# All gathered expert rows on VectorE, the dot rows first, and a row in every second group left over

## What is computed

```
q = (xb @ w_q).reshape(blk, PEER_HEADS, 2, PEER_QDIM // 2)
s = einsum("thpd,pnd->thpn", q, keys)
sv, si = top_k(s, 16)
cand = sv[:, :, 0, :, None] + sv[:, :, 1, None, :]
cidx = si[:, :, 0, :, None] * 128 + si[:, :, 1, None, :]
best, pos = top_k(cand.reshape(...), 16)
eidx = take_along_axis(cidx..., pos)
g = softmax(best)
act = gelu(einsum("thkd,td->thk", u_tab[eidx], xb))
y = einsum("thk,thkd->td", g * act, v_tab[eidx])
```

## Time and profile before

| | |
|---|---|
| median of 3 runs | 5243.1 us (5241.55 to 5251.99) |
| the profiled execution's own time | 5246.87 us |
| its span | 5245.1 us |
| TensorE busy | 92% of the span |
| VectorE busy | 56% |
| ScalarE busy | 20% |
| GpSimd busy | 35% |
| mean DMA rate | 284 GB/s |

### The profile page before, as it was taken

One profiled execution on the slowest core, in us unless ns is written; L12 is line 12 of the kernel. 1 busy time (PEld: TensorE's weight loads), 2 busy tenths in 40 slices (PEclk: granted clock), 3 DMA queues, 4 the chain that ended last, 5 costly groups with the idle time before them and its releaser, 6 DMA issues.

```text
span 5245.1 us, 84061 instructions
## 1 busy us (share of the span) xinstructions
PE 4838.5 (92%) x25356; PEld 3800.1 (72%) x25356; DVE 2943.4 (56%) x5545; ACT 1067.2 (20%) x2624; POOL 1860.3 (35%) x2605
## 2 busy tenths in 40 slices
PE   7999899788999988999989998987889999989998
PEld 5887776567877765777768877764678777757776
DVE  2543332424789787666436433323348896876664
ACT  1112111210111367100011121112101114680000
POOL 4430000324554445454245200003236543454442
PEclk9999999889999999999999999998999999999999
DMA  7753679487789999999877437895768898989997
GB/s 275 246 177 115 201 239 320 139 263 241 266 304 339 342 366 329 383 409 412 328 274 245 164 114 219 250 308 159 249 212 297 307 344 335 377 321 391 413 405 283
DMA packets 723471, 1489.24 MB, mean 284 GB/s; under 512 B 64592, under 2 KB 405584, under 8 KB 721568
## 3 DMA queue, kind: packets, MB, share of 16 engines
q0 software_dynamic: 249888, 858.18, 44.5%
q1 hardware_dynamic: 473216, 626.61, 35.9%
HBM read 1315.99 MB, written 302.75 MB: 309 GB/s over the span
## 4 chain that ended last, share of the span: by engine, by line
PE 61%; DMA 13%; issue 9%; DVE 8%; DVEq 3%; SPq 2%; POOLq 2%; POOL 1%; ACT 1%; ACTq 0%
PE PS L1357 19%; PE PS L694 10%; PE PS L798 8%; DMA xT<-u_rows,arena 6%; PE PS L1232 3%; PE PS L1300 3%; PE PS L925 3%; DVE xT L1960 2%; PE PS L1251 2%; PE PS L1256 2%; DMA hT<-u_rows,arena 1%; PE PS L837 1%; DMA xT<-v_rows,arena 1%; DMA u_rows<-arena 1%; DVE arena L1995 1%
## 5 line engine op out<-in xcount | busy, mean ns | idle before, releaser
L1300 PE MATMUL PS<-hT,ring 128*128 128x288 f32 x4096 | 1014.5, 408 | 17.0 <-DMA ring<-in_uv 17.0
L1357 PE MATMUL PS<-arena,ring 128*128 128x288 f32 x4096 | 994.5, 406 | 1.0 <-DMA ring<-in_uv 1.0
L1300 PEld LDWEIGHTS PS<-hT,ring 128*128 128x128 f32 x4096 | 775.2, 191 | 224.9 <-issue 17.9
L1357 PEld LDWEIGHTS PS<-arena,ring 128*128 128x128 f32 x4096 | 778.2, 190 | 217.0 <-DMA ring<-in_uv 1.9
L565 POOL DMA_DIRECT2D u_rows<-arena x1024 | 564.5, 553 | 144.5 <-DVE arena L1507 63.6
L798 PE MATMUL PS<-hT,ring 128*128 128x272 f32 x2304 | 604.6, 409 | 5.9 <-DMA ring<-in_wst 5.9
L673 POOL DMA_INDIRECT xT<-u_rows,arena x410 | 416.4, 1016 | 457.9 <-DVE arena L1960 386.2
L1969 DVE SCALAR_TENSOR_TENSOR PS<-xT,arena,PS 128x1024 f32<-128x1024 f32 x344 | 443.4, 1289 | 215.4 <-DMA xT<-v_rows,arena 205.2
L1960 DVE CUSTOM_DVE_ANT_0 xT<-xT,PS 128x1024 f32<-128x1024 f32 x410 | 495.0, 1216 | 104.6 <-DMA xT<-u_rows,arena 103.8
L2178 ACT ACTIVATE arena<-PS 128x272 f32<-128x272 f32 (+12 forms) x540 | 207.6, 395 | 1520.1 <-PE PS L798 533.5
L798 PEld LDWEIGHTS PS<-hT,ring 128*128 128x128 f32 x2304 | 438.6, 198 | 99.0 <-issue 16.6
(11 more groups left out here) (399 smaller groups left out, 5920.9 us busy)
## 6 DMA issues: line engine op xcount, KB each, us to landing
ring<-in_uv SPq DMA_DIRECT2D x512, 512.0 KB, 6.4
ring<-in_wst SPq DMA_DIRECT2D x312, 512.0 KB, 5.5
u_rows<-arena POOLq DMA_DIRECT2D x1024, 128.0 KB, 4.6
v_rows<-in_uv SPq DMA_DIRECT2D x256, 512.0 KB, 6.6
arena<-in_uv POOLq DMA_DIRECT2D x216, 512.0 KB, 6.2
arena<-in_ck SPq DMA_DIRECT2D x128, 256.0 KB, 5.1
arena<-in_cvv POOLq DMA_DIRECT2D x64, 256.0 KB, 4.3
hT<-in_cvv POOLq DMA_DIRECT2D x64, 256.0 KB, 5.5
```

What stands on the lines that cost most here:

```text
L1300: i = mm(PS[:, 2 + s % 2, 0:TD], ring[:, s, c, :], hD[:, c, :], start=(c == 0), stop=(c == DC - 1))
L1357: i = mm(PS[:, 2 + b, 0:TD], ring[:, s, j, :], WB[:, row, :], start=(row == 0), stop=(row == NK - 1))
```

## The change

Three things are changed, all in PEER and the same in both layers.

1. `T_ROWS` is gone: TensorE treats no gathered row, ScalarE makes no diagonal, and the order of the rows is simply all u rows of block 0, all of block 1, then all v rows of block 0 and of block 1. All 512 are VectorE's.
2. Beside the U pass, VectorE's comparison for the next group stands right behind `weighted` of this one, ahead of the gathered rows that follow it.
3. In the 28 groups left over VectorE does one row in every second group: 14 rows in all, where there were 28 on VectorE and 28 on TensorE.

```diff
-    order = u[0] + u[1][:N_EARLY]
-    for g in range(N_LEFT):
-        order += [v[0][g], u[1][N_EARLY + g]]
-    return order + u[1][N_EARLY + N_LEFT:] + v[0][N_LEFT:] + v[1]
+    return u[0] + u[1] + v[0] + v[1]
...
                 if n >= NBUF:
-                    used = row_t if on_tensor(n - NBUF) else row_v
-                    g.wait_ge(used.sem, used.at(l, RANK[n - NBUF]))
+                    g.wait_ge(row_v.sem, row_v.at(l, n - NBUF + 1))
...
             for g in range(N_IN_U, N_OH):
                 one_hots(g)
-                r = g - N_IN_U
-                n = T_ROWS[r]
-                pe.wait_ge(row_ld[n % NBUF].sem, row_ld[n % NBUF].at(l, 16 * (n // NBUF + 1)))
-                pe.nop(nofuse=True)
-                pe.wait_ge(dg_s.sem, dg_s.at(l, r + 1))
-                pe.nop(nofuse=True)
-                for hf in range(2):
-                    i = mm(HTK[0][:, hf, :], DG[r % 2], row_buf(n)[:, hf * 512:(hf + 1) * 512], start=(r == 0), stop=(r == N_LEFT - 1))
-                i.then_inc(row_t.sem, 1)
...
+            onehots(0)
             for m in range(I_OH, NK):
                 g = m - I_OH
-                onehots(g)
                 rows(first + (P + N_EARLY - first) * (2 * g + 1) // (2 * N_IN_U))
...
                 weighted(g, m)
+                onehots(g + 1)
                 rows(first + (P + N_EARLY - first) * (2 * g + 2) // (2 * N_IN_U))
-            v.wait_ge(dot_s.sem, dot_s.at(l, 1))
-            v.nop(nofuse=True)
-            tt(DOT[:, 0:P], DOT[:, 0:P], GW[:, 0:P], ALU.mult)
-            v.drain().then_inc(dot_v.sem, 1)
-            onehots(N_IN_U)
             for g in range(N_IN_U, N_OH):
                 if g + 1 < N_OH:
                     onehots(g + 1)
                 weighted(g, NK - 1)
-                row()
+                if g % 2:
+                    row()
...
-            rows(RANK[N_SW + NBUF + 1])
+            rows(N_SW + NBUF + 2)
...
             row_onehots(N_IN_U)
             row_onehots(N_IN_U + 1)
-            s_.wait_ge(dot_v.sem, dot_v.at(l, 1))
-            for r in range(N_LEFT):
-                if 0 < r < N_LEFT - 1:
-                    row_onehots(N_IN_U + r + 1)
-                if r >= 2:
-                    s_.wait_ge(row_t.sem, row_t.at(l, r - 1))
-                act(DG[r % 2], ident[:, :], ACT.Copy, scale=DOT[:, r:r + 1]).then_inc(dg_s.sem, 1)
+            for g in range(N_IN_U + 2, N_OH):
+                row_onehots(g)
             activated(1)
```

More of the change, by code:

```diff
@@ L173 @@
 N_IN_U = NK - I_OH
-N_LEFT = N_OH - N_IN_U
 ROWS = row_order()
@@ L177 @@
 N_SW = (NROW - 12) // NBUF * NBUF
[L178 to L182, removed]
+LAST = {key: max(n for n, r in enumerate(ROWS) if r[:2] == key) + 1 for key in (("u", 0), ("u", 1), ("v", 0))}
 def shape_constants():
@@ L282, in build @@
     row_buf = lambda n: (ROW_X if n < N_SW else ROW_W)[n % NBUF]
-    DG = [xflat[:, 4 * DM + P * i:4 * DM + P * (i + 1)] for i in range(2)]
     YD = [hflat[:, TD * c:TD * (c + 1)] for c in range(DC - 1)]
@@ L411, in build @@
     row_ld = [Sig(f"expert_row_loaded{b}", 16 * len(range(b, NROW, NBUF))) for b in range(NBUF)]
-    row_v, row_t = Sig("row_used_by_vector", len(V_ROWS)), Sig("row_used_by_tensor", len(T_ROWS))
-    dot_s, dot_v, dg_s = Sig("dots_activated", 2), Sig("first_row_weights_ready", 1), Sig("row_diagonal_ready", N_LEFT)
+    row_v = Sig("row_used", NROW)
+    dot_s = Sig("dots_activated", 2)
     xk_st, xr_ld = Sig("x_kept", 16), Sig("x_loaded_again", 16)
@@ L1946, in row @@
                 nonlocal at
-                n = V_ROWS[at]
+                n = at
                 at += 1
@@ L1963, in row @@
                 else:
-                    if blk == 0 and k == N_LEFT:
-                        v.wait_ge(row_t.sem, row_t.at(l, N_LEFT))
-                        v.nop(nofuse=True)
                     v.wait_ge(row_v.sem, row_v.at(l, at - 1))
@@ L2162, in _ @@
                 v.drain()
-                rows(min(at + 1, len(V_ROWS)))
+                rows(min(at + 1, NROW))
             gathered_out(0)
-            rows(len(V_ROWS))
+            rows(NROW)
             v.drain().then_inc(ya_v.sem, 1)
@@ L2441, in activated @@
                 cols = slice(GCOL[blk], GCOL[blk] + P)
-                s_.wait_ge(row_v.sem, row_v.at(l, LAST_DOT[blk]))
+                s_.wait_ge(row_v.sem, row_v.at(l, LAST["u", blk]))
                 act(DOT[:, cols], DOT[:, cols], ACT.Gelu_apprx_tanh).then_inc(dot_s.sem, 1)
@@ L2462, in _ @@
                 dense_kept(c)
-            s_.wait_ge(row_v.sem, row_v.at(l, RANK[ROWS.index(("v", 0, P - 1))]))
+            s_.wait_ge(row_v.sem, row_v.at(l, LAST["v", 0]))
             copy(YT[0], htk(0)).then_inc(ya_s.sem, 1)
```

## The result

The changed kernel takes 5288.8 us (median of 4 runs, 5285.8 to 5296.9), the one before, run beside it, 5246.8 us (5241.6 to 5252.0): a ratio of 1.0089, 95% interval 1.0077 to 1.0102. It is slower by about 42 us. Its profiled execution took 5291.5 us, with a span of 5289.9 us.

What follows compares the result with a forecast made beforehand. TensorE was taken to bound the kernel, except where it waits for weights and gathered rows. Per layer -16 + 2 - 3 + 38 = +21, twice +42, plus 1 for the second layer's clock: 5286 us, 8-in-10 range 5250 to 5312.

Steps and rivals of the forecast that it cites:

- The groups left over: Stage between U and V pass: at ScalarE's pace of 2.89 us a group, the V pass begins 15.9 us earlier, -16 a layer.
- the rival of hand-overs at the lower clock: Groups left over: hand-overs between three engines set the 3.36 us pace, so the stage gets no shorter, 5314 us; chance 0.10.
- the comparison ... is ready before ScalarE's factor: First group left over: VectorE's comparison, moved ahead of two rows, comes early, so ScalarE is the last to arrive.
- some 82 us: Sign in the later profile: V pass begins this long behind the U pass's end, where it was 101.7 us.
- TensorE's clock: V pass's beginning: TensorE stays at the lower clock through the groups left over, costing half of about 4 us, +2 a layer.
- Beside the U pass: During the U pass: comparison ahead of the rows saves little, -3 a layer, with bounds 0 and -22.
- takes away what TensorE waits for: Beside the U pass: the moved comparison removes TensorE's waits for it, at most 21.9 us a layer.
- its doubt behind it: Beside the U pass: VectorE still has the same rows, each behind its transfer, so only its wait for ScalarE's copy is saved.
- The rows that are moved: V pass and layer's end: 267 rows instead of 226, row 500 done at V + 505, layer ends V + 540, +38.
- The early signals: V pass: row 384 at V + 288, needed by V + 312, hidden by 24 us; TensorE stalls from 2.07 us a row.
- go round as fast as loaded DMA engines let them: V pass: loaded DMA engines limit how fast the five row buffers are reused, at 1.914 us a row.
- The break-even of 1.81 us: V pass: pace per row at which row 500 is done at V + 484, where the change neither gains nor loses.

Runs made afterwards that it cites:

- e11: e6 with eight more 128 x 128 products on TensorE, result unread, behind the one-hot products of each group left over: 5215.1 us, ratio 0.9928 to the kernel before.
- e6: Changed kernel with 42 rows on VectorE among the groups left over, where it had 14: 5215.7 us, ratio 0.9944 to the kernel before.
- e1: Kernel before with only the comparison moved ahead of the gathered rows beside the U pass: 5239.5 us against 5248.1, ratio 0.9984.
- e3: Changed kernel without the last 42 v rows of block 1, neither fetched nor added, in both layers: 5209.3 us against 5248.1 for the kernel before.
- e7: Changed kernel with four row buffers instead of five: 5567.6 us against 5249.4 for the kernel before, ratio 1.0606.
- e9: Changed kernel with a sixth row buffer from row 225 on: 5275.3 us against 5251.8 for the kernel before, ratio 1.0045.
- e4: Changed kernel loading only half of each V tile, TensorE's work unchanged: 5217.9 us against 5248.1 for the kernel before, ratio 0.9942.
- e8: Changed kernel loading only an eighth of each V tile, TensorE's work unchanged: 5206.5 us in one run.

## Why the prediction was right

The predicted time was 5286 us, the measured one is 5288.8: a slowdown of 43 us was forecast, against the median of 5243.1, and 42 came. That the two agree to 1 us is luck, since the kernel before alone had medians from 5243.1 to 5251.8 us; the terms are what counts. Point by point, per layer (first, second):

- *The groups left over*, -16: measured -13.8 and -15.2. ScalarE's pace is the 2.89 us that two groups of the earlier trace rows had shown, and the rival of hand-overs at the lower clock fell: TensorE did stay at the lower clock, and the pace held. The step that failed is "the comparison ... is ready before ScalarE's factor". It was the last to arrive, behind rows that stand before the last `weighted` (the timeline above): TensorE began at 2021.4, 1.9 us behind the factor, and so ScalarE waited 1.11 us ahead of its third group. That is about half of the first layer's miss of 2.1 us; the rest is small gaps and a last hand-over longer than the 0.6 us taken. (The "some 82 us" that the prediction gives as a sign does not follow from its own sum: 101.7 - 15.9 is 85.8.)
- *TensorE's clock*, +2: the stage ran at 0.54 and the V pass began at the lower clock, and it was 1.1 us longer than before in either layer (499.7 and 499.4 against 498.6 and 498.3). In the timeline of the V pass's first microseconds (TensorE's busy time, clock, DMA):

```profile
2104.00:2106.00 2.00, 2.00 (x6) 0.50 0.34 39
2106.00:2108.00 2.00, 2.00 (x9) 0.83 0.78 281
```

  Against e11, whose V pass begins at the higher clock, the term is 1.6 to 2.1 us by the length of the V pass in e6.
- *Beside the U pass*, -3: 232.2 and 230.6 us from first to last group, where it was 236.2 and 233.6, so -4.0 and -3.1. The prediction's sentence that the edit "takes away what TensorE waits for" failed, and its doubt behind it held: most of the waits stayed. In the changed kernel, the waits from 1782 to 2015 us, and one of them on VectorE and on TensorE:

```profile
PE PS L1302 <- DVE hT L2090: 18.8, 18, 2.2
```

```profile
1899.31 0.59 DVE L2099 TENSOR_TENSOR arena<-arena,PS 128x424 f32<-128x424 f32 x1
1899.82 0.68 DVE L2090 TENSOR_TENSOR hT<-iota,RO 128x512 f32<-128x512 f32 x1
1900.86 1.13 PE L1302 MATMUL PS<-hT 128*128 128x128 f32 x8 [1.02 <-DVE hT L2090]
```

  The comparison comes late because the `weighted` ahead of it does, and that one had stood behind three gathered rows, two of which had waited for their transfers (0.96 and 0.22 us). e1 says the same: the new order gives 3 to 6 us a layer, not 22.
- *The rows that are moved*, +38: V + 542.6 and V + 540.5 against V + 502, so +41 and +39, which holds what the lower clock cost as well. Row 500 was done at V + 507.5 and V + 503.8, forecast V + 505; row 505 began at V + 518.2 and V + 516.0, forecast V + 514; from there it took 24.4 us in both, forecast 26.2. The pace was 1.90, forecast 1.914. Two parts were off and nearly cancelled: the return of x with what hangs on it took 10.7 and 12.2 us where 9 was taken, and the end 1.8 less. The last rows were mis-sized too, for a reason the prediction had not seen. It let them run alone at 1.4 us each. But in the first layer SyncE goes straight on to the next layer's tiles: it issues the first ones at 2593.4, V + 490.6, and from 2602 to 2610 us, when TensorE is already idle, the transfers still get 418 GB/s (the two lines below). The last ten rows up to row 500 took 1.88 us each there, and 1.64 in the second layer, where no tiles follow. e3 shows that without the 42 rows nothing of the term is left.

```profile
2593.44 9.57 SPq L445 DMA_DIRECT2D ring<-in_wst  x4
2602.00:2610.00 8.00, 0.51 (x3) 0.05 (x1) 5.88 (x5) 0.00 (x0) 4.09 (x5) 0.69 1.03 418
```

- *The early signals* cost nothing, as forecast: TensorE was idle for 0.7 us in the whole V pass. Row 384 was done at V + 287.2 and V + 284.2, forecast V + 288, and e7 shows the stall that was forecast for a slower pace.
- Between the first layer's end and the second's first group 5.5 us more went than before, where 1 was forecast for the clock. In the experiments' traces this stretch is anything from 1761 to 1777 us, whatever was changed, so nothing is made of it; nor of the first layer's first group, which came 4.2 us earlier than before.

The stretches that the change touches sum to +22.9 and +20.6 us, where +21 was forecast for each. With the two stretches that it doesn't touch, -4.2 and +5.5, the profiled executions differ by +18.8 and +26.0.

One sentence of the prediction holds only in part: the buffers "go round as fast as loaded DMA engines let them". The pace was right since it was read and not derived. A buffer less slows it (e7), a buffer more gives next to nothing (e9), and fewer bytes beside it give 6 and 11% (e4, e8); two limits at one point fit that, as said above, but are not shown. The break-even of 1.81 us lies just above what e4 had, 1.78, and e4 was indeed faster than before, by 30 us where that pace gives under 20 by the prediction's own terms. The Trainium skill's ceiling of 436 GB/s (page "DMA: Bandwidth & Descriptors", section "Where 436 GB/s comes from") was not reached in any stretch shown here; 416 over 300 us was the most, in e9. The prediction's estimate from it, 1.74 us a row and a kernel at 5221 us, did not come true: with full tiles the pace was 1.875 us at best.

## What to carry to other kernels

When work that runs under another engine's stage is shifted to it, count the stage's slack first, in units of that work at the pace it has there: here 27.6 us of slack held 14 rows at 1.9 us, and 42 were put in. A place where the needed resource lies idle is worth filling to just beyond the point where the filler becomes the limit: in the groups left over the DMA engines were at 0.42, a row cost VectorE 1.3 us where it cost 1.9 later, and 42 rows there made the better kernel than 14 or 28. A wait for an operation is not shortened by its length when the operation is moved ahead in its engine's program, if what now stands ahead of it is as late: of 22 us for the comparison, moving it gave 3 to 6.

## What the runs showed of the hardware

The DMA share is no measure of how much room is left. It was 0.97 at 361 GB/s with half the V tile bytes, 0.96 at 352 GB/s with four buffers, and 1.02 at 411 to 416 GB/s with full tiles. A share near 1 at 360 GB/s was thus not the ceiling; the same engines gave 55 GB/s more. One reason is in the rows of the gathers' queue above: the same bytes were counted with 14% more time in e8 than in the changed kernel. What did point to a ceiling was asking for more: a sixth buffer raised the rate from 411 to 416 GB/s and no further.

In the groups left over of the changed kernel, with one group's products every 2.89 us and about 0.84 us of idle time behind each, TensorE was granted 0.54 over 87 us, that is nearly all of it at 1.2 GHz; in e11, where the added products, 1.95 us of them, follow each group's, it was granted 0.96, nearly all of it at 2.4 GHz.
